# A mixture-of-experts layer: rows gathered for two experts at a time, and the token products split in two

## The reference

```python
logits = (h @ w_router) + b_router
top_v, top_i = lax.top_k(logits, TOP_K)          # 4 of 32
gates = jax.nn.softmax(top_v, axis=-1)
# for every expert e and the tokens that chose it:
xb = h[toks]
gu = xb @ w_gu[e] + b_gu[e]                      # 1024 x 2048
gate = jnp.minimum(gu[:, :D_FF], SWIGLU_LIMIT)
up = jnp.clip(gu[:, D_FF:], -SWIGLU_LIMIT, SWIGLU_LIMIT)
act = gate * jax.nn.sigmoid(gate * SWIGLU_ALPHA) * (up + 1.0)
y = act @ w_down[e] + b_down[e]                  # 1024 x 1024
y = y * gw[:, None]                              # added to its tokens
```

## Time and profile before

| | |
|---|---|
| runs without a profile | 1046.61, 1047.21, 1051.9 us; median 1047.21 |
| the profiled execution, its own time | 1052.23 us |
| its span, first to last instruction | 1050.4 us |
| mean granted clock of PE | 0.987 of full |
| PE busy | 1014.1 us, 97% |
| PEld busy | 453.2 us, 43% |
| DVE, ACT, POOL busy | 211.3, 147.5, 16.9 us |
| read from HBM | 416.35 MB, 397 GB/s over the span |

### The profile page before, as it was taken

One profiled execution on the slowest core, in us unless ns is written; L12 is line 12 of the kernel. 1 busy time (PEld: TensorE's weight loads), 2 busy tenths in 40 slices (PEclk: granted clock), 3 DMA queues, 4 the chain that ended last, 5 costly groups with the idle time before them and its releaser, 6 DMA issues.

```text
span 1050.4 us, 12608 instructions
## 1 busy us (share of the span) xinstructions
PE 1014.1 (97%) x5069; PEld 453.2 (43%) x5069; DVE 211.3 (20%) x620; ACT 147.5 (14%) x273; POOL 16.9 (2%) x12
## 2 busy tenths in 40 slices
PE   5889999999999999999999999999999999999997
PEld 3455544444443444444444443344444444434443
DVE  1655411111111111111111111111111111101112
ACT  0331211011111111111101111111111101101111
POOL 0050000000000000000000000000000000000000
PEclk9989799999999999999999999999999999999999
DMA  9994599999999999999999999999999999999991
GB/s 326 339 353 153 212 410 427 429 427 426 427 428 428 429 429 428 427 429 429 427 429 429 427 429 429 429 427 428 429 429 426 411 426 426 429 428 428 427 395 47
DMA packets 41772, 417.84 MB, mean 398 GB/s; under 512 B 8336, under 2 KB 9104, under 8 KB 17072
## 3 DMA queue, kind: packets, MB, share of 16 engines
q1 hardware_dynamic: 36672, 415.91, 94.8%
q10 hardware_dynamic: 5072, 1.51, 0.8%
HBM read 416.35 MB, written 1.05 MB: 397 GB/s over the span
## 4 chain that ended last, share of the span: by engine, by line
PE 90%; DVE 6%; ACTq 3%; ACT 1%; issue 1%
PE ps L989 44%; PE ps L1056 22%; PE ps L953 13%; PE ps L967 6%; DVE PT L765 2%; PE ps L859 2%; PE ps L1032 2%; ACTq L426 1%; ACTq L421 1%; ACT PR L464 1%; PE ps L1073 0%; ACTq L418 0%; PE ps L839 0%; DVE passing L621 0%; PE ps L930 0%
## 5 line engine op out<-in xcount | busy, mean ns | idle before, releaser
L989 PE MATMUL ps<-ring,PT 128*64 128x512 f32 x2008 | 450.6, 596 | 0.5 <-ACT PT L505 0.5
L989 PEld LDWEIGHTS ps<-ring,PT 128*64 128x64 f32 x2008 | 142.2, 137 | 288.9 <-issue 286.5
L1056 PE MATMUL ps<-ring,PT 128*64 128x512 f32 x1020 | 225.9, 595 | 5.7 <-DVE PT L765 5.7
L753 DVE TENSOR_SCALAR tT<-ps 128x256 f32<-128x256 f32 x64 | 27.2, 425 | 686.5 <-PE ps L989 686.5
L953 PEld LDWEIGHTS ps<-qk,N 128*128 128x128 f32 x1056 | 130.1, 200 | 21.1 <-issue 21.1
L953 PE MATMUL ps<-qk,N 128*128 128x64 f32 x1056 | 134.4, 287 | 0.0
L1056 PEld LDWEIGHTS ps<-ring,PT 128*64 128x64 f32 x1020 | 70.3, 137 | 141.2 <-issue 128.1
L512 ACT ACTIVATE tT<-tT 128x256 f32<-128x256 f32 x64 | 26.7, 416 | 466.7 <-DVE tT L753 466.7
L967 PE MATMUL ps<-PT 64*128 64x512 f32 x256 | 63.6, 615 | 0.8 <-ACT PT L518 0.8
L518 ACT COPY PT<-ps 128x512 f32<-128x512 f32 x32 | 18.7, 585 | 221.1 <-PE ps L1056 221.1
L512 ACT ACT_TABLE_LOAD x32 | 41.1, 1283 | 0.6
(11 more groups left out here) (158 smaller groups left out, 330.3 us busy)
## 6 DMA issues: line engine op xcount, KB each, us to landing
ring<-w_gu_dram SPq DMA_DIRECT2D x121, 2048.0 KB, 21.9
ring<-w_down_dram SPq DMA_DIRECT2D x61, 2048.0 KB, 24.0
ring<-w_gu_dram SPq DMA_DIRECT2D x9, 1024.0 KB, 21.0
ring<-w_down_dram SPq DMA_DIRECT2D x8, 512.0 KB, 20.6
ring<-w_in_dram SPq DMA_DIRECT2D x8, 384.0 KB, 7.7
ring<-w_in_dram SPq DMA_DIRECT2D x2, 1024.0 KB, 13.3
ring<-w_out_dram SPq DMA_DIRECT2D x1, 2048.0 KB, 19.1
ring<-w_out_dram SPq DMA_DIRECT2D x2, 1024.0 KB, 22.3
```

The lines of the kernel that those rows point to most:

```text
L753: nc.vector.tensor_scalar(gb[:, b, :], gu[:, b, 0, :], LIMIT, None, ALU.min).then_inc(g_ready, 1)
L989: last = mm(ps[64 * j:64 * j + 64, GU + b, :].rearrange("p (f n) -> p f n", f=2), lhs, halves[j][:, :, 256 * b:256 * b + 256], start=start ...
L1056: last = mm(ps[64 * j:64 * j + 64, DWN, :], aT[:, k, 64 * (c - GU_PIECES):64 * (c - GU_PIECES) + 64], rows[:, 512 * j:512 * j + 512], star ...
```

## The change

`gather` now works on a pair of experts. DVE builds S1 for two experts side by side (128 columns, four operations, every second expert). PE gathers half of the chunks (4 of 8) for both experts of the next pair while it is at one expert, and the other half at the next: 128 moving columns, half as many matmuls per expert. Two `xe` buffers take turns. The first of them is PR[:, 0], the second the upper half of `passing`; both held early loads before, so `AHEAD` goes from 5 to 4, that is 8 half chunks, and SP's early loads change places with their waits. The first pair is gathered ahead of the experts, in two halves, the second into the bank LOGITS.

The token products no longer stand behind the first gate/up piece: those of token tile 0 now stand between the gather and the activation's transposes, those of tile 1 between these transposes and the ones of SG. The waits for `gt_sb` and `y_sb` stand ahead of the gather.

ACT and DVE, which looped over single experts, now loop over turns of four, as PE did.

```diff
-AHEAD = 5
+AHEAD = 4
@@ tiles
-        xe = cut(KC * SLOTS, of).rearrange("p (k s) -> p k s", k=KC)
-        S1 = cut(T * SLOTS, of).rearrange("p (t s) -> p t s", t=T)
+        S1 = cut(T * P, of).rearrange("p (t s) -> p t s", t=T)
-            mixA[:, :, :].rearrange("p h s -> p (h s)"), PR[:, 0, :], X[:, 0, :], w2b, X[:, 1, :],
-            passing[:, 0:1024], passing[:, 1024:2048])]
+            mixA[:, :, :].rearrange("p h s -> p (h s)"), X[:, 0, :], w2b, X[:, 1, :], passing[:, 0:1024])]
+        xe = [half.rearrange("p (k s) -> p k s", k=KC) for half in (PR[:, 0, :], passing[:, 1024:2048])]
@@ SP
             load_ahead(3)
-            load_ahead(4)
             sp.wait_ge(opened, 1)
             sp.wait_ge(h_ss, 1)
             sp.wait_ge(n2_sb, 1)
+            load_ahead(4)
+            sp.wait_ge(n2_sb, T)
             load_ahead(5)
-            sp.wait_ge(n2_sb, T)
+            sp.wait_ge(opened, T)
             load_ahead(6)
-            sp.wait_ge(opened, T)
+            sp.wait_ge(sg_ready, 1)
             load_ahead(7)
-            sp.wait_ge(sg_ready, 1)
-            load_ahead(8)
-            load_ahead(9)
@@ ACT
-            act.wait_ge(gathered, 1)
-            nc.scalar.copy(xe, ps[:, GAT, :].rearrange("p (k s) -> p k s", k=KC)).then_inc(xe_sb, 1)
+            for h, bank in enumerate((GAT, LOGITS)):
+                act.wait_ge(gathered, h + 1)
+                nc.scalar.copy(xe[0][:, 4 * h:4 * h + 4, :], ps[:, bank, :].rearrange("p (k s) -> p k s", k=4)).then_inc(xe_sb, 1)
...
-                act.wait_ge(gathered, n + 2)
-                nc.scalar.copy(xe, ps[:, GAT, :].rearrange("p (k s) -> p k s", k=KC)).then_inc(xe_sb, 1)
+                act.wait_ge(gathered, n + 3)
+                rows = xe[(u // 2 + 1) % 2][:, 4 * (u % 2):4 * (u % 2) + 4, :]
+                nc.scalar.copy(rows, ps[:, GAT, :].rearrange("p (k s) -> p k s", k=4)).then_inc(xe_sb, 1)
@@ DVE
             def build_s(n):
+
                 for t in range(T):
-                    ins = nc.vector.tensor_scalar(S1[:, t, :], iota[:, 0:SLOTS], rank[:, t, bass.ds(n, 1)], None, ALU.is_equal)
+                    for i in range(2):
+                        ins = nc.vector.tensor_scalar(S1[:, t, i * SLOTS:(i + 1) * SLOTS], iota[:, 0:SLOTS], rank[:, t, bass.ds(n + i, 1)],
+                                                      None, ALU.is_equal)
                 ins.then_inc(s_ready, 1)
...
-                dve.wait_ge(gathered, n + 1)
-                build_s(n + 1)
+                if u % 2 == 0:
+                    dve.wait_ge(gathered, n + 2)
+                    build_s(n + 2)
@@ PE
-            def gather(n):
-
-                pe.wait_ge(s_ready, n + 1)
-                for k in range(KC):
+            def gather(pair, h, bank=GAT):
+
+                pe.wait_ge(s_ready, pair + 1)
+                for k in range(4 * h, 4 * h + 4):
                     for t in range(T):
...
-                        last = mm(ps[:, GAT, k * SLOTS:(k + 1) * SLOTS], rows, S1[:, t, :], start=t == 0, stop=t == T - 1)
+                        last = mm(ps[:, bank, (k - 4 * h) * P:(k - 4 * h + 1) * P], rows, S1[:, t, :], start=t == 0, stop=t == T - 1)
...
-            gather(0)
+            gather(0, 0)
+            gather(0, 1, LOGITS)
...
-                pe.wait_ge(xe_sb, n + 1)
+                pe.wait_ge(xe_sb, turn * TURN + 2 * (u // 2) + 2)
+                mine = xe[u // 2][:, :, SLOTS * (u % 2):SLOTS * (u % 2 + 1)]
...
-                    if c == 0 and step != "first":
-                        pe.wait_ge(gt_sb, n)
-                        pe.wait_ge(y_sb, n)
-                        to_tokens()
...
-                gather(n + 1)
+                if step != "first":
+                    pe.wait_ge(gt_sb, n)
+                    pe.wait_ge(y_sb, n)
+                gather(turn * 2 + u // 2 + 1, u % 2)
+                if step != "first":
+                    to_tokens(0)
                 pe.wait_ge(act_ready, n * 2 + 2)
...
                 last.then_inc(aT_psum, 1)
-                pe.wait_ge(xe_sb, n + 2)
+                if step != "first":
+                    to_tokens(1)
+                pe.wait_ge(xe_sb, n + 3)
                 pe.wait_ge(sg_ready, n + 1)
```

More of the change, by code:

```diff
@@ L518, in expert, with turn_of_experts @@
                 nc.scalar.copy(ye, ps[:, DWN, :]).then_inc(y_sb, 1)
-            with act.Fori(0, NE) as e:
-                expert(e)
-            more_passes(act, NE, lambda p, e: expert(p * NE + e))
+            def turn_of_experts(n):
+                for u in range(TURN):
+                    expert(n + u, u)
+            with act.Fori(0, TURNS) as r:
+                turn_of_experts(r * TURN)
+            more_passes(act, TURNS, lambda p, r: turn_of_experts(p * NE + r * TURN))
             for t in range(T):
@@ L746, in _, with expert @@
             gu = ps[:, GU:GU + 2, :].rearrange("p b (f n) -> p b f n", f=2)
-            def expert(n, e):
-                dve.wait_ge(gathered, n + 1)
-                build_s(n + 1)
+            def expert(n, e, u):
+                if u % 2 == 0:
+                    dve.wait_ge(gathered, n + 2)
+                    build_s(n + 2)
                 for b in range(2):
@@ L767, in expert, with turn_of_experts @@
                 build_sg(n + 1)
-            with dve.Fori(0, NE) as e:
-                expert(e, e)
-            more_passes(dve, NE, lambda p, e: expert(p * NE + e, e))
+            def turn_of_experts(n, e):
+                for u in range(TURN):
+                    expert(n + u, e + u, u)
+            with dve.Fori(0, TURNS) as r:
+                turn_of_experts(r * TURN, r * TURN)
+            more_passes(dve, TURNS, lambda p, r: turn_of_experts(p * NE + r * TURN, r * TURN))
             for t in range(T):
@@ L963, in _, with to_tokens @@
             pe.wait_ge(count_ready, 1)
-            def to_tokens():
-                return [[mm(ps[:, ACC[t] + j, :], GT[64 * j:64 * j + 64, t, :], ye[64 * j:64 * j + 64, :],
-                            start=False, stop=True, skip_group_check=True) for j in range(2)] for t in range(T)]
+            def to_tokens(t):
+                return [mm(ps[:, ACC[t] + j, :], GT[64 * j:64 * j + 64, t, :], ye[64 * j:64 * j + 64, :],
+                           start=False, stop=True, skip_group_check=True) for j in range(2)]
             def expert(turn, u, step=None, early=None):
@@ L1011, in expert @@
                         if 2 * c + k < KC - 1:
-                            last = gate_up(xe[:, 2 * c + k, :], halves, c + k == 0, False)
+                            last = gate_up(mine[:, 2 * c + k, :], halves, c + k == 0, False)
                     if c < GU_PIECES - 1:
                         last.then_inc(pieces_used, 1)
-                    if c == 0 and step != "first":
-                        pe.wait_ge(gt_sb, n)
-                        pe.wait_ge(y_sb, n)
-                        to_tokens()
                 pe.wait_ge(oneh_ready, n + 1)
                 for b in range(2):
-                    last = gate_up(xe[:, KC - 1, :], halves, False, False, [b])
+                    last = gate_up(mine[:, KC - 1, :], halves, False, False, [b])
                     if b == 1:
@@ L1088, in _ @@
             pe.wait_ge(y_sb, NE)
-            for tile in to_tokens():
-                for last in tile:
+            for t in range(T):
+                for last in to_tokens(t):
                     last.then_inc(acc_final, 1)
```

2 lines of the change are left out of this document (1 added, 1 removed).

## The result

The changed kernel takes 1039.61 us (median of 4 runs, 1037.89 to 1041.29), the kernel before in the same comparison 1049.56 (1046.61 to 1052.93): a ratio of 0.9888, 95% interval 0.9839 to 0.9937. The prediction was 1037.7 us, and 9.5 us less than before; measured are 9.95 us between the medians (the interval allows 6.6 to 16.9). The profiled execution took 1038.21 us.

A forecast was written before the change was run, and what follows sets the result against it. PE bound the kernel at 28.54 us an expert, DMA 3% behind; afterwards the queue binds. Start +0.35, bytes +2.45 and shorter work behind the last landing: span 1050.4 - 9.5 = 1040.9, median 1047.21 to 1037.7 us; range 1031 to 1046.

The forecast's parts named there:

- Start of the refills: Before expert 0's first refill: DVE's four operations instead of two in build_s delay the queue's start by 0.35 us.
- Bytes: Weight queue: one 1 MiB chunk less preloaded, so 1.049 MB more in the bound stretch at 427 GB/s, +2.45 us.
- Behind the last landing: Last expert: weights land at 1029.4, down matmuls end at 1033.6 (before 1043.1), then an unchanged tail of 7.3 us.
- The last wait: Last expert: PE waits last for the final gate/up half piece, landing at 1019.2 us.
- PE's period: PE's work per expert: 28.54 less 1.9 for gather and 0.65 for split tokens, 26.0 us.
- the gather: Gather on PE: 16 records of 128 columns per expert instead of 32 of 64, at 0.119 us, saving 1.9 us.
- The split: Token products between transposes and down matmuls: the second half covers DVE's copy of aT, saving 0.65 us per expert.
- any average below 28.8 us per expert gives it: Whole expert loop: the forecast time hardly depends on PE; any average pace below 28.8 us gives the same 1037.7 us.
- rival D: Gather on PE saves nothing, 128 columns costing twice 0.119; PE needs 27.9 us, same time as forecast; no separate chance.
- A: Last expert or start pays more, at half clock or in the first gather: 1041.2 to 1044.7 us; chance 0.17.
- B: Expert loop: PE's clock falls again and again after waits for weights, 29.3 us an expert, 1066 us; chance 0.06.
- C: Weight queue runs faster when asked for more, say by 2%: bytes take 875 us instead of 893, time 1020; chance 0.02.

The follow-up runs named there:

- experiment 6: Changed kernel with the first chunk of every refilled gate/up piece not loaded (result differs): 851.6 us from first refill to end of span.
- experiments 3: Changed kernel with six early half chunks instead of eight: 911.3 us from first refill to end, ratio 0.9903 to the kernel before.
- experiment 4: Kernel before with eight early half chunks instead of ten: 920.1 us from first refill to end, ratio 1.0009 to the kernel before.
- experiment 2: Changed kernel with token products put back behind the first gate/up piece, pair gather kept: 908.3 us from first refill to end, ratio 0.9887.
- experiment 1: Kernel before with only the token products split as in the changed kernel: 918.5 us from first refill to end, ratio 0.9978.
- experiments 8: Changed kernel with all of each gather's matmuls issued twice: 917.3 us from first refill to end, ratio 0.9990 to the kernel before.
- Experiment 9: Kernel before with split token products, early half chunks used for experts 12 to 16 instead of 24 to 28: 912.4 us from first refill, ratio 0.9935.
- experiments 7: Changed kernel with half of every gather's matmuls issued a second time: 912.2 us from first refill to end, ratio 0.9937.

## Why the prediction was right, and where it was not

**The bound changed hands as foretold.** PE's idle before gate/up, the lag that climbs and stands at 33 us, waits from the ninth expert on (341 us; "after 8 or 9 experts" was forecast), unchanged GB/s: each is in the profile after. The size of the gain came from bytes and the queue's start, not from the 67 us (32 x 2.1) that PE saved. The sum by its terms:
- Start of the refills, forecast +0.35 us. In the traces it is 2.88 earlier, by chance: in the first trace of the kernel before, the first gather ran at half clock, while in nine of the other thirteen traces the clock was 1.00 there and in four it was down for less (means of 0.74 to 0.91 in 112 to 132 us, 0.66 in the first). The windows of both kernels from 120 to 132 us (busy times, then granted clock):

```profile
120.00:132.00 12.00, 11.55 (x47) 6.08 (x48) 0.42 (x2) 2.12 (x3) 0.00 (x0) 0.65 0.34 105
```

```profile
120.00:132.00 12.00, 11.34 (x64) 5.96 (x64) 1.61 (x7) 2.71 (x4) 0.00 (x0) 1.00 0.56 187
```

  Counted from the issue of piece 6, ahead of that, the first refill comes after 36.5 us in the three traces with the old front at full clock (36.54, 36.53, 36.52) and after 36.9 to 37.0 with the new one (36.92, 36.90, 36.92, 37.00; a fifth, experiment 6, has 37.90): +0.4. That the forecast span of 1040.9 was 4.5 too long comes from this lottery: the before trace was a late one. That the forecast of the time was 1.9 too short comes from another: the median of the kernel before moved from 1047.21 to 1049.56 with one run more. Both are luck; the stretch is the fairer measure, and the difference in it is 9.3 us at equal clock (918.5 to 909.25).
- Bytes, forecast +2.45 us at the last landing. Measured +0.8 to +1.1 (897.2 and 897.5 for 896.4), while the step by itself is +2.1 (experiments 3, 4). The 1.0 to 1.3 us between the two do not come from the queue's start. Counted from the first refill, the first 50 us bring as much in the kernel before as in the changed one:

```profile
130.19:180.19 50.00, 49.31 (x264) 22.38 (x262) 9.44 (x28) 5.45 (x10) 0.00 (x0) 1.00 0.99 412
```

```profile
127.31:177.31 50.00, 49.37 (x248) 20.39 (x246) 9.17 (x28) 4.75 (x10) 0.00 (x0) 1.00 0.99 413
```

  Nor do they come from the 800 us behind that. With the same bytes (the changed kernel and experiment 4) the down weights of the last but one expert land 862.7 and 862.9 us (changed, both traces) and 862.9 us (experiment 4) behind the first refill, and only with the next piece, the last expert's first, is it 872.3 and 872.7 against 873.7. What holds that piece up by a microsecond is open.
- Behind the last landing, forecast 4.2 us to the end of the down matmuls, measured 4.8; tail 7.1 for 7.3. From the first refill to the end: forecast 910.4, measured 909.1 and 909.4.
- The last wait. The forecast let PE wait last for the second half of the last gate/up piece. It waited last for the third piece; of the fourth, PEld waited 0.47 us for the second half (until 1014.44) and PE not at all.
- PE's period, forecast 26.0 us, measured 26.43: 2.11 saved for 2.55, and the waits 2.9 us an expert (29.37 - 26.43) for 3.4. The end does not depend on it.
- Of this the gather, forecast 1.9 us an expert: 16 records at 0.125 us, 1.74 saved. Twice the columns beneath the weight load cost 5% more, nearly nothing, as the equal cadence of the earlier trace rows had it.
- The split, forecast 0.65 us: 0.61 in the changed kernel (experiment 2), for which it was forecast, and 0.28 on the kernel before (experiment 1). In both each half costs 1.07 us, so two cost 2.13 where eight in a row took 1.92, and 0.21 go back. The two savings don't just add up: the gather alone is worth 1.50 us (28.54 to 27.04), since the hole behind it grows, and the split then fills it.

**The step that failed is "any average below 28.8 us per expert gives it"**, and with it rival D, which held that a PE at 27.9 us would end at the same time. At equal clock the change gains 9.3 us; at 28.26 and 28.32 us 1.7 and 1.2 of them are left (experiments 1, 8), at 27.04 all (experiment 2), and at 27.38 somewhere from 6.3 to all, by how much of the 912.2 is put down to the clock. The formula took PE and queue as two totals, of which the larger counts. But the ring lets the queue lag by 33 to 35 us at most. If that limit is met in the middle, PE waits; and if behind it, over the early chunks, the queue needs only 27.0 us an expert (29.4 less the 2.45 of a megabyte), a PE of 28.3 falls behind the queue and the waits are lost. By this working the condition is a pace below that of the queue in the last stretch, about 27.0, or a relief placed where no wait arises; the runs put the limit between 27.04 and 28.26. The change's 26.4 is below it, so the forecast stood; by the working the margin was 0.6 us an expert and not 2.4. Experiment 9 shows the mechanism from the other side. A PE at 27.9, rival D's, was not run.

The count of ring and queue that stands in the expectations of experiments 7 to 9 (piece by piece, 4.91 us each, eight slots, PE's measured pace) was on record before those runs: 911.0, 920.6 and 913.6, measured 912.2, 917.3 and 912.4. It took in 1.6 us for the fall of the clock, which experiments 8 and 9 did not have. It is thus good to 1 or 2 us, enough to tell the gain from none. Such a count needs only a pace, so one could have been made beside the prediction; that it would have caught the step then is argued, not shown.

**The rivals.** A and B, the clock: the granted clock is 1.00 in all windows from 145 to 801 us, with 1.2 us waits in every expert from the ninth on, so waits of that size do no harm here, like the one of 1.26 us in the earlier trace rows; the Trainium skill's warning (TensorE: Matmul & The Clock Gate, HAM oscillation) of loops that turn cold at every wait for a chunk does not come true with waits this short. One sign of A and B did fire: the clock is below 1 from 916 to 922 us (0.71, 0.50, 0.94), with PE busy throughout, so not by the waits that A and B blamed, and at no cost. From 945 us to the end it is 1.00 again. C: the rate stayed at 427 to 429 GB/s with the lag at its limit; the 435 of the Trainium skill (DMA: Bandwidth & Descriptors, Specifications) was not reached.

**Open.** What makes the front vary before 95 us, and whether a stretch at half clock hits the first gather more often in one kernel than in the other.

## What to carry to other kernels

Two resources at 97% and 100% mean that a saving on the first is worth only what the second leaves, and the growth of the landing lag per iteration tells how much that is. But don't compare totals: walk the buffer through the stages, since a wait in the middle is lost for good when the waiting engine is the slower one afterwards, and early-loaded bytes belong ahead of the place where the lag would meet the buffer's limit. When the front of a kernel varies more than the change, measure from a mark behind it, and before crediting the rest to the change see that the clock did the same in both traces. A DMA rate is compared between kernels in windows counted from that mark too, not from the start.

## What the runs showed of the hardware that was not expected

- 128 moving columns cost hardly more than 64 under a 128x128 f32 weight load at full clock too: 0.125 us a record for 0.119.
- Eight records of 64-row matmuls took 1.92 us in one group and 2.13 in two groups of four.
- PE's clock fell without any idle time. Behind the down-bias products (L1073, 3.7 us, with a stationary operand of 32 rows) eight of the fourteen traces have the granted clock below 1.00 for some us, down to 0.50, and six have not. That the 32 rows are the reason is not shown. It is why the two traces of the kernel before differ by 1.7 us in the stretch (5.46 for 3.77 us across the products); the same 6 us of work, in the first and in the second (busy times, then granted clock):

```profile
926.00:932.00 6.00, 6.00 (x19) 1.61 (x17) 0.00 (x0) 0.00 (x0) 0.00 (x0) 0.72 0.98 418
```

```profile
922.00:928.00 6.00, 6.00 (x27) 1.91 (x25) 0.00 (x0) 0.00 (x0) 0.00 (x0) 1.00 1.01 431
```

  Where the queue binds it costs nothing (909.1 with it at 0.60 from 916 to 920 us, 909.4 with it at 0.50 from 920 to 926).
- Issued 1.7 us early into an empty queue, half a piece brought 0.7 us (one trace each).
